# Latent norms begun one product earlier and spread over steps, modulation steps begun five steps behind their loads, in a two-block fp32 kernel

## What is computed

```python
# first block
hn = rmsnorm(h, mix_norm_g)
q_a, k_a, v_a, cq, ckv, k_pe = split(hn @ w_in)          # k_pe: the rotary keys, 64 wide
q  = rmsnorm(cq, cq_g) @ w_q_up                          # cq 512 wide, 8 heads of 192
kv = rmsnorm(ckv, ckv_g) @ w_kv_up                       # ckv 256 wide
out_b = softmax(rope(rmsnorm(q)) @ rope(rmsnorm([k, k_pe])).T) @ v
out_a = neighbourhood_attention(q_a, k_a, v_a)           # with bias and a column mask
h = h + concat(rmsnorm(out_a), rmsnorm(out_b)) @ w_out
h = h + conv_glu(rmsnorm(h))                             # gate, up, down; 5632 wide
# second block: everything is modulated by the vector c
sh_m, sc_m, gt_m, sh_f, sc_f, gt_f = split(silu(c) @ w_ada + b_ada)   # 2048 x 12288
x = x + gt_m * (merged(rmsnorm(x) * (1 + sc_m) + sh_m) @ w_o)
x = x + gt_f * glu(rmsnorm(x) * (1 + sc_f) + sh_f)
```

## Time and profile before

| | |
|---|---|
| median of 3 runs | 2782.65 us (2779.78 to 2783.17) |
| profiled execution | 2776.33 us, span 2775.0 us |
| PE busy | 2682.7 us (97%), weight loads 2638.7 us (95%) |
| DVE / ACT / POOL busy | 1800.6 (65%) / 1214.8 (44%) / 321.6 us (12%) |
| mean granted PE clock | 0.985 of full speed |
| DMA | 571.18 MB, 206 GB/s on average |

### The profile page before, as it was taken

One profiled execution on the slowest core, in us unless ns is written; L12 is line 12 of the kernel. 1 busy time (PEld: TensorE's weight loads), 2 busy tenths in 40 slices (PEclk: granted clock), 3 DMA queues, 4 the chain that ended last, 5 costly groups with the idle time before them and its releaser, 6 DMA issues. The chain is left out here.

```text
span 2775.0 us, 51102 instructions
## 1 busy us (share of the span) xinstructions
PE 2682.7 (97%) x22036; PEld 2638.7 (95%) x22036; DVE 1800.6 (65%) x2489; ACT 1214.8 (44%) x1861; POOL 321.6 (12%) x533
## 2 busy tenths in 40 slices
PE   7899989899999999998999999999899999999998
PEld 6888879899999999998999999999899999999997
DVE  5656567877777777775788667767554454444454
ACT  4456544544433444434444443334444443344442
POOL 1110113211111111221000001111100000000001
PEclk9999999999999999999999999999999999999999
DMA  6343457688888787885444568887545555555553
GB/s 198 119 118 91 125 178 230 216 266 272 271 280 284 267 274 267 273 275 175 152 152 148 180 224 275 270 278 244 166 164 186 188 181 184 194 192 187 182 186 118
DMA packets 500001, 571.18 MB, mean 206 GB/s; under 512 B 26688, under 2 KB 473280, under 8 KB 499776
## 3 DMA queue, kind: packets, MB, share of 16 engines
q1 hardware_dynamic: 467968, 463.76, 51.2%
q0 software_dynamic: 31520, 103.36, 11.4%
q10 hardware_dynamic: 288, 0.80, 0.1%
HBM read 565.77 MB, written 2.54 MB: 205 GB/s over the span
## 5 line engine op out<-in xcount | busy, mean ns | idle before, releaser
L1596 DVE TENSOR_TENSOR wl<-raw,wh 128x1024 fp32r<-128x1024 f32 (+1 forms) x894 | 1060.3, 1204 | 675.3 <-ACT wh L1143 669.8
L575 PE MATMUL ps<-xx,wh 128*128 128x256 f32 (+2 forms) x5104 | 1459.2, 286 | 39.3 <-DVE xx L1651 18.1
L576 PE MATMUL ps<-xx,wh 128*128 128x256 f32 (+2 forms) x5104 | 1439.1, 282 | 0.0
L577 PE MATMUL ps<-xx,wl 128*128 128x256 f32 (+2 forms) x5104 | 1435.7, 281 | 0.0
L1143 ACT ACTIVATE wh<-raw 128x1024 fp32r<-128x1024 f32 (+1 forms) x894 | 880.9, 1029 | 639.0 <-PE ps L577 631.3
L575 PEld LDWEIGHTS ps<-xx,wh 128*128 128x128 f32 x5104 | 967.2, 190 | 49.4 <-issue 30.2
L576 PEld LDWEIGHTS ps<-xx,wh 128*128 128x128 f32 x5104 | 968.4, 190 | 1.7 <-issue 1.0
L577 PEld LDWEIGHTS ps<-xx,wl 128*128 128x128 f32 x5104 | 967.7, 190 | 0.0
L575 PE MATMUL ps<-hid,wh 128*128 128x256 f32 x1408 | 394.0, 280 | 0.0
L576 PE MATMUL ps<-hid,wh 128*128 128x256 f32 x1408 | 393.6, 280 | 0.0
L577 PE MATMUL ps<-hid,wl 128*128 128x256 f32 x1408 | 392.8, 279 | 0.0
(11 more groups left out here) (300 smaller groups left out, 1949.4 us busy)
## 6 DMA issues: line engine op xcount, KB each, us to landing
raw<-in_w_in SPq DMA_DIRECT2D x118, 1024.0 KB, 5.2
ada_raw<-in_w_ada POOLq DMA_DIRECT2D x384, 256.0 KB, 4.8
raw<-in_w_gate SPq DMA_DIRECT2D x44, 1024.0 KB, 6.7
raw<-in_w_up SPq DMA_DIRECT2D x44, 1024.0 KB, 7.1
raw<-in_w_ffn_gate SPq DMA_DIRECT2D x44, 1024.0 KB, 5.0
raw<-in_w_ffn_up SPq DMA_DIRECT2D x44, 1024.0 KB, 5.1
raw<-in_w_down SPq DMA_DIRECT2D x32, 1024.0 KB, 6.7
raw<-in_w_ffn_down SPq DMA_DIRECT2D x32, 1024.0 KB, 5.5
```

The lines of the kernel that those rows point to most:

```text
L575: pe.matmul(dst, h[:, c, o:o + w], x[:, 0, k, g.t0:g.t1], start=(k == 0), stop=False)
L576: pe.matmul(dst, h[:, c, o:o + w], x[:, 1, k, g.t0:g.t1], start=False, stop=False)
L577: m = pe.matmul(dst, l[:, c, o:o + w], x[:, 0, k, g.t0:g.t1], start=False, stop=end)
L1596: dve.tensor_tensor(wl[i % NS][:, part], raw[i % NR][:, part], wh[i % NS][:, part].bitcast(F32), ALU.subtract).then_inc(s_lo, 1)
```

## The change

The loads, sums and tiles stay the same; three things are moved.

- `latent` starts ahead of the product of the rotary keys on all four engines, and the squares, the sums and the roots stand in different steps: squares of `cq` in step 1, their sum on PE in step 3, root and reciprocal of `cq` and the squares of `ckv` in step 4, scaling of `cq` in step 5, the sum of `ckv` in step 6, its root in step 7, its scaling in step 8. Before, the squares and sum and root of one norm all stood in one step. Steps 1 to 4 are the quarters of the `kpe` slab, 5 to 8 those of the first slab of `q0`. `key_rope` starts where it did.
- ACT and DVE wait, ahead of the squares, until ACT has written `cq` and `ckv` out of their banks.
- `ada` on PE, DVE and POOL pauses for `ADA_LEAD` = 5 slow steps instead of one between the first three loads and the first step.

```diff
+ADA_LEAD = 5
@@ tensor_program
             def latent():
-                yield
+                yield from pause(2)
                 pair_sums(N_CQ)
-                yield
-                yield
+                yield from pause(3)
                 pair_sums(N_CKV)
                 yield
@@
             gemm(("ckv", 0))
+            lanes.start("latent", latent())
             gemm(("kpe", 0))
-            lanes.start("latent", latent())
             lanes.start("key_rope", key_rope())
@@ gpsimd_program
             def latent():
-                yield
-                yield
+                yield from pause(4)
                 yield from norm_lows(N_CQ)
-                yield
+                yield from pause(2)
                 yield from norm_lows(N_CKV)
@@ scalar_program
             def latent():
-                yield
                 pair_squares(N_CQ)
+                yield from pause(3)
                 root(N_CQ)
+                pair_squares(N_CKV)
                 yield
                 yield from norm_his(N_CQ, 0)
-                pair_squares(N_CKV)
+                yield
                 root(N_CKV)
                 yield
                 yield from norm_his(N_CKV, 0)
@@ vector_program
             def latent():
-                yield
                 pair_squares(N_CQ)
+                yield from pause(3)
                 reciprocal(N_CQ)
+                pair_squares(N_CKV)
                 yield
                 yield from norm_scales(N_CQ)
-                pair_squares(N_CKV)
+                yield
                 reciprocal(N_CKV)
                 yield
                 yield from norm_scales(N_CKV)
@@
-            for key in (("cq", 0), ("cq", 1), ("ckv", 0), ("kpe", 0)):
+            for key in (("cq", 0), ("cq", 1), ("ckv", 0)):
                 gemm(key)
+            lanes.start("latent", latent())
+            gemm(("kpe", 0))
@@ ada on PE, DVE and POOL
-                yield
+                yield from pause(ADA_LEAD)
                 for i in range(24 * 16):
```

More of the change, by code:

```diff
@@ L1189, in pair_squares @@
                         act.wait_ge(s_h[2 * i // 4], 16)
+                    if n == N_CQ and i == 0:
+                        for g in range(2):
+                            for j in range(2):
+                                act.wait_ge(*last_use(("cq", g), j))
+                    if n == N_CKV:
+                        for j in range(2):
+                            act.wait_ge(*last_use(("ckv", 0), j))
                     if i >= len(bufs):
@@ L1626, in pair_squares @@
                         dve.wait_ge(s_h[(2 * i + 1) // 4], 16)
+                    if n == N_CQ and i == 0:
+                        for g in range(2):
+                            for j in range(2):
+                                dve.wait_ge(*last_use(("cq", g), j))
+                    if n == N_CKV:
+                        for j in range(2):
+                            dve.wait_ge(*last_use(("ckv", 0), j))
                     if i >= len(bufs):
```

## The result

| | median, us (range, runs) | profiled execution, us | its span |
|---|---|---|---|
| before | 2781.24 (2779.78 to 2783.17, 4) | 2776.33 | 2775.0 |
| changed | 2761.69 (2758.68 to 2762.48, 4) | 2762.48 | 2761.2 |

What follows compares the result with a forecast made beforehand. TensorE, busy 97% of the span, was taken as the bound, so only its waits and slow clock could be had. 6.4 + 4.4 + 2.8 = 13.6 us off gave 2762.7 profiled, median 2769, range 2762 to 2779.

Steps and rivals of the forecast that it cites:

- The first and second sum: Latent norms: PE's two waits for the sums of squares, 2.8 and 3.3 us, go, the first to within 0.1.
- The rotation's wait: Rotary keys in the first query slab: PE waits anew 2.15 us (1.7 to 3.3) for DVE's key scaling.
- The clock at the latent norms: Two slow stretches of 1.7 us each behind the old waits go; 0.85 us is charged behind the new wait.
- The start of the modulation: Softmax waits near 392 and 408 us: 2.6 and 0.9 us off, 0.9 of clock, together 4.4 us (2.6 to 6.4).
- The end: Last modulation sum at 1926.5 us: wait 1.3 instead of 3.04, 1.7 us gained, plus 1.1 of clock.
- I price this at zero: The 22 other transpositions, moved from `up` to `gate` slabs and the like, bring no wait: zero us.
- The deadlines lie far behind: Modulation groups: the deadlines at 8, 12, 20 and 24 groups are far off from steps two slabs later.
- rival D: Moved transpositions at `gate` slab ends meet a late DVE, 8 of 24 wait: 16 us slower, 2799; chance 0.03.
- A: The rotation's wait takes most of the latent part, modulation pays only at its start: 7 us, 2776; chance 0.22.
- C: Waits come back elsewhere on DVE, only some 3 us stay: 2780; chance 0.07.
- B: No rotation wait, both slow stretches vanish, all modulation waits and clock go: 20.5 us, 2762; chance 0.10.
- The sum: Whole kernel: 6.4 + 4.4 + 2.8 = 13.6 us off, median forecast at 2769 us.

Runs made afterwards that it cites:

- again: The changed kernel with no edit, run once more against the kernel before: ratio 0.9938, median 2762.1 us.
- endonly: The changed kernel with one pause step before the first modulation step and the other four ahead of step 208: ratio 0.9957, median 2766.4 us.
- ada: The kernel before with only the modulation part of the change (five steps of pause): ratio 0.9968 to the kernel before, median 2769.2 us.
- beforetwo: The kernel before with no edit, run and traced a second time: ratio 1.0001, median 2777.9 us.
- keyseven: The changed kernel with the key's scaling ahead of the four scalings of cq and 7 pause steps for 5: ratio 0.9939 to before, median 2762.1 us.
- latent: The changed kernel with ADA_LEAD = 1, so the latent part alone: ratio 0.9966 to the kernel before, median 2769.8 us.
- leadtwo: The changed kernel with ADA_LEAD = 2 in place of 5: ratio 0.9952 to the kernel before, median 2766.4 us.
- keyfirst: The changed kernel with the key's scaling ahead of the four scalings of cq on DVE: ratio 0.9923 to the kernel before, median 2758.5 us.
- ropelate: The changed kernel with six DVE zero writes, some 2 us, ahead of the key's scaling: ratio 0.9951 to the kernel before, median 2765.9 us.

## Why the prediction was right, and where it was off

**The first and second sum** (all 6.1 us gone): right. DVE has the second pair of additions done at 72.2 and PE doesn't wait.

**The rotation's wait** (2.15 us): 2.11, by the chain as worked out. DVE of the changed kernel:

```profile
78.06 0.96 DVE L1604 TENSOR_TENSOR wl<-raw,wh 128x768 fp32r<-128x768 f32 x1 [1.23 <-ACT wh L1143]
78.94 1.28 DVE L1683 SCALAR_TENSOR_TENSOR nx<-cq,vec,rstd 128x258 f32<-128x258 f32 x3
80.14 0.42 DVE L1666 TENSOR_TENSOR cqx<-nx,cqx 128x258 fp32r<-128x258 f32 x1
80.47 0.87 DVE L1683 SCALAR_TENSOR_TENSOR sqt<-cq,vec,rstd 128x258 f32<-128x258 f32 x1
81.27 0.35 DVE L1714 TENSOR_SCALAR kpe<-kpe,vec 64x272 f32<-64x272 f32 x1
```

The fourth scaling takes 0.87 us again, as in the earlier trace rows, and the key's scaling starts behind it at 81.27; the forecast's 80.1 is 1.1 us earlier, as all of this execution is at this place.

**The clock at the latent norms**: here the step failed. It took 3.4 us of loss as the price of the old waits and 0.85 as that of the new one. By the table (1 less the clock, times 22 us) the three traces with the old waits lose 3.5, 1.8 and 3.5 us, and the six with the rotation's wait of 2.1 lose 3.5, 1.8, 1.8, 1.8, 0 and 3.5, 2.1 on average (2.9 for the three). So the clock gives back some 0.8 us rather than 2.55. In the profiled pair it gave back nothing, and the part came to 4.4 us up to `qup` 0 in place of 6.4; in `again`, with 0.92 there, it came to 5.9; between all traces with the old order and all with this wait it is 5.4. By the rule of the Trainium skill weighed in the prediction (TensorE: Matmul & The Clock Gate, "HAM oscillation — how this bites in real kernels"), that PE pays again each time it idles, one stretch would stay and the part give 5.5 us, an estimate; the traces agree with it on average (5.4), not one by one (4.4 and 5.9).

**The start of the modulation** (4.4 us): right. 4.5 between kernels that differ in this part alone (`endonly` and the changed kernel, 41.8 and 37.3 us from `outb` 0 to 4), 4.8 by the slabs of the profiled pair, 4.3 to 6.5 by the times of `endonly`. The waits were forecast at 0 and 1.2 us and are 0.57 and 0.80. The first doesn't vanish, because PE too comes earlier by then. The clock was put at even odds and is a clear case: 0.87 or 0.96 in all four traces with a first step behind one pause, 1.00 in all ten with more.

**The end** (2.8 us): 3.95 by the slabs; 3.4 between the averages of three traces and six; 3 us by difference (8.9 of `ada` less the start's 5.9). The wait is 0.64 us where 1.3 was forecast. PE and DVE of the changed kernel:

```profile
1929.22 0.66 PE L675 MATMUL ps<-cst,ada_acc 128*128 128x128 f32 x4 [0.64 <-DVE ada_acc L1813]
```

```profile
1921.18 0.87 DVE L1846 SCALAR_TENSOR_TENSOR H<-ps,mod,H 128x256 f32<-128x256 f32 x2
1923.48 1.42 DVE L1604 TENSOR_TENSOR wl<-raw,wh 128x1024 fp32r<-128x1024 f32 x1 [1.44 <-ACT wh L1143]
...
1928.42 0.74 DVE L1813 SCALAR_TENSOR_TENSOR ada_acc<-ada_raw,small,ada_acc 128x512 f32<-128x512 f32 x1
```

The wait for ACT (1.44) and the three splits and steps (5.7 us, 1923.48 to 1929.16) are as estimated from the earlier trace rows; PE reached the sum 6.5 us behind the residual's end (1929.22 less 0.64, less 1922.05), not the 5.6 of the forecast. Its slow stretch is gone, of which two thirds had been taken; but `beforetwo` has none there either (1.00 behind a wait of 2.7 us), so the stretch was never sure to be paid.

**"I price this at zero"** for the 22 moved transpositions: right; no wait at a `gate` slab, and rival D falls. **"The deadlines lie far behind"**: the one sentence that was wrong and cost nothing here. `mod_until(20)` is at most two steps away, as `keyseven` shows.

**The rivals**: A and C ask for waits that come back; besides the rotation's, 0.9 us did, at the FFN's norm, and cost no time. B forecast 2762 and the median is 2761.7, so B has the number; but its reason is wrong: the rotation does wait, and the clock behind it is not gone.

**The sum** was 13.6 us against 13.85 in the profiled pair, and the median was forecast at 2769 and is 2761.7, 7 us lower and below the band of 2766 to 2773 that the forecast was given. That the pair agrees is luck, on two sides. The trace before was of a quick execution: against `beforetwo` the changed kernel's span is 20.6 us shorter. And the sum is closer than its terms deserve: latent 2.0 short, start 0.4 and end 1.15 over, and three items that it didn't have, 2.6 us of gain at the norm of 370 to 386 us, and losses of 1.1 us ahead of the first product and of 1.4 between 98 and 370. The runs say 17 to 18 us. The 4 us between are about what this one execution lost beside the change, against a quick one of the kernel before: 1.1 ahead of the first product, 1.4 between 98 and 370 us, and 1.4 by a clock behind the rotation that lost 3.5 us where the mean of six is 2.1. In `again` the last two are not there (-0.7 us between 98 and 370, and 1.8 behind the rotation).

The gain at the norm of 370 to 386 us is not shown to be the change's. Its wait is 2.6 us in all 14 traces, and `ada` changes nothing ahead of it and has 0.89. The kernel before has ten slow microseconds behind it in both traces, and so has `keyseven`, whose fixed stretch (0.79) shows only the rest of them, since its norm comes 7 us earlier. The kernel before and `keyseven`, columns as above:

```profile
372.00:383.00 11.00, 10.79 (x48) 10.03 (x49) 9.76 (x12) 6.64 (x17) 9.12 (x12) 0.54 0.22 68
...
366.00:377.00 11.00, 10.46 (x48) 9.69 (x47) 9.77 (x11) 6.38 (x17) 8.88 (x11) 0.53 0.30 95
```

Nor does it cost its length. From `outb` 0 to 4 the kernel before takes 2.9 us more than `latent`, which has no slow stretch at the norm, and `keyseven` 1.5 to 1.9 more than the kernels with five and nine steps; and with five steps a stretch of 3.4 us there (changed kernel) or none (`again`) gives the same 37.3 us: without it PE waits 1.3 us for DVE's work, which it doesn't in the changed kernel:

```profile
PE ps L702 <- DVE na1k L1796: 1.3, 1, 1.3
```

## What to carry to other kernels

When the engine that sets the time waits for a chain on another, look first whether producer and consumer stand one step apart in the same round, and move them apart; starting earlier without that was worth nothing here. Work that is put off still has its deadline: follow the last step before each one, since five steps of delay gained 9 us here and nine gave 6 to 7 of them back. And price a wait by a run that changes it alone, and read it between the starts of the same two slabs: totals of one execution hold several microseconds of slow clock that lie elsewhere the next time, and a stretch of fixed microseconds shows another piece of the kernel in every variant.

## What the runs showed of the hardware

- The clock behind a short wait isn't fixed by the program. Behind the same wait of 2.1 us the granted clock over 22 us was 0.84 (changed kernel), 0.92 (the same kernel again), and 1.00 (`leadtwo`).
- It needs no long wait: of eleven traces with 2.1 us or more of waiting there ten had a lowered clock, of the three without any none had. In `keyfirst` the clock fell at 103 us, beside a wait of 1.15 us for GpSimd (0.86 from 100 to 112 us).
- At the same clock a microsecond of such a wait cost a microsecond (2.4 us of `ropelate`'s more at 0.84, 2.2 for 2.1 us at 1.00), and at the same wait each further slow stretch of 3.4 us cost 1.5 us (21.8, 23.3 and 24.8 us from the key slab to `qup` 0).
- A slow stretch costs time only where PE sets the pace: behind the norm at 370 us one of 3.4 us cost nothing (37.28 us with it, 37.30 without, from `outb` 0 to 4), and one of ten cost 2.9 us (44.7 against 41.8).
- Behind that norm's wait, 2.6 us in all 14 traces, five had no slow stretch, six one of 3.4 us and three one of ten, of them both of the kernel before. What decides it is open.
